# The two top weight blocks of each group of products in one transfer of 1 MB instead of two of 512 KB

## The reference

```python
proj = _rms(x, norm_mix) @ w_in          # 2048 x 4096: u | B | C | v
u, bg, cg, v = split(proj)
ya = pool_mixer(u)                       # trailing means over windows 2, 4, 8, 16, minus the token, times w_pool
yb = bg * conv3_causal(cg * v)
x = x + concat([ya, yb]) @ w_out
x = x + cross_attention(_rms(x, norm_attn), memory)
x = x + square(relu(_rms(x, norm_mlp) @ w_up)) @ w_down      # w_up 2048 x 8192, w_down 8192 x 2048
```

## Time and profile before

| | us |
|---|---|
| median of 3 runs | 2612.54 (2611.84 to 2614.34) |
| the profiled execution's own time | 2611.28 |
| its span, first to last instruction | 2609.6 |
| PE busy | 2569.2 (98%) |
| DVE busy | 1914.0 (73%) |
| ACT busy | 1107.6 (42%) |
| granted TensorE clock | 0.998 of full |

### The profile page before, as it was taken

The page is one execution under the profiler, slowest core; times in us unless marked ns, Lnnn a source line. Parts: engine busy times, 40 slices in busy tenths (PEclk is TensorE's granted clock), DMA queues, the critical chain, the costliest instruction groups (busy, mean ns, idle before and its releaser), DMA issues.

```text
span 2609.6 us, 47588 instructions
## 1 busy us (share of the span) xinstructions
PE 2569.2 (98%) x20056; PEld 2514.8 (96%) x20056; DVE 1914.0 (73%) x2342; ACT 1107.6 (42%) x1520; POOL 159.9 (6%) x253
## 2 busy tenths in 40 slices
PE   8999999999999999999999999999999999999997
PEld 8989999999999989989999999999999999999997
DVE  6789887763542243368888888888878888888888
ACT  6444444441321122234656555555533333333344
POOL 1000000010000010000011111000010000000000
PEclk9999999999999999999999999999999999999999
DMA  8673333362233455532566666565587555556542
GB/s 282 210 216 121 106 102 110 109 220 86 88 121 116 152 194 195 217 98 100 170 221 221 221 221 209 192 226 195 187 304 275 183 200 191 194 192 211 192 137 101
DMA packets 131856, 462.51 MB, mean 177 GB/s; under 512 B 11952, under 2 KB 18224, under 8 KB 120400
## 3 DMA queue, kind: packets, MB, share of 16 engines
q1 hardware_dynamic: 92448, 260.05, 30.8%
q0 software_dynamic: 39216, 199.71, 20.7%
HBM read 376.62 MB, written 83.09 MB: 176 GB/s over the span
## 4 chain that ended last, share of the span: by engine, by line
PE 92%; DVE 4%; issue 1%; DMA 1%; ACT 1%; SPq 0%; DVEq 0%; ACTq 0%
PE psum_main L2577 27%; PE psum_main L2187 25%; PE psum_side L2577 20%; PE psum_main L2322 7%; PE psum_side L2322 5%; PE psum_main L2298 3%; PE psum_main L2431 1%; DMA unit_raw<-weights 1%; PE psum_main L2503 1%; DVE unit_low L1865 1%; PE psum_side L2472 1%; PE psum_side L2396 1%; ACT unit_high L1161 1%; DMA mem_raw<-mem_t 0%; DVE residual L1998 0%
## 5 line engine op out<-in xcount | busy, mean ns | idle before, releaser
L1161 ACT ACTIVATE unit_high<-unit_raw 128x1024 fp32r<-128x1024 f32 x384 | 400.7, 1055 | 531.9 <-PE psum_main L2577 158.4
L1865 DVE TENSOR_TENSOR unit_low<-unit_raw,unit_high 128x1024 fp32r<-128x1024 f32 x384 | 468.0, 1222 | 108.2 <-ACT unit_high L1161 107.9
L2577 PE MATMUL psum_main<-tokens,unit_high 128*128 128x272 f32 x2048 | 388.5, 288 | 4.8 <-DVE hidden L1968 3.7
L2577 PE MATMUL psum_main<-hidden,unit_high 128*128 128x272 f32 x1984 | 377.0, 288 | 3.7 <-DVE residual L1998 2.7
L791 ACT ACTIVATE unit_high<-unit_raw 128x1024 fp32r<-128x1024 f32 x162 | 171.0, 1058 | 438.6 <-PE psum_main L2187 398.5
L2187 PE MATMUL psum_main<-inner_a,unit_high 128*128 128x272 f32 x2080 | 348.1, 289 | 2.8 <-issue 2.8
L2577 PEld LDWEIGHTS psum_main<-tokens,unit_high 128*128 128x128 f32 x2048 | 321.8, 189 | 5.6 <-DVE hidden L1968 4.4
L2577 PEld LDWEIGHTS psum_main<-hidden,unit_high 128*128 128x128 f32 x1984 | 312.1, 189 | 4.8 <-DVE residual L1998 3.7
L2187 PEld LDWEIGHTS psum_main<-inner_a,unit_high 128*128 128x128 f32 x2080 | 294.3, 188 | 6.1 <-issue 5.9
L2577 PE MATMUL psum_main<-tokens,unit_low 128*128 128x272 f32 x1024 | 295.1, 288 | 0.0
L2577 PE MATMUL psum_side<-tokens,unit_high 128*128 128x272 f32 x1536 | 293.1, 288 | 1.4 <-issue 0.8
(11 more groups left out here) (285 smaller groups left out, 4694.8 us busy)
## 6 DMA issues: line engine op xcount, KB each, us to landing
unit_raw<-weights SPq DMA_DIRECT2D x442, 512.0 KB, 4.3
hidden<-hidden_kept POOLq DMA_DIRECT2D x56, 1088.0 KB, 6.8
hidden_kept<-hidden_staged POOLq DMA_DIRECT2D x31, 1904.0 KB, 7.4
unit_sum<-weights SPq DMA_DIRECT2D x40, 512.0 KB, 3.6
residual<-x_t POOLq DMA_DIRECT2D x16, 544.0 KB, 5.9
residual_kept<-residual POOLq DMA_DIRECT2D x32, 272.0 KB, 5.0
cache_ring_t<-cache_k POOLq DMA_DIRECT2D x8, 1024.0 KB, 7.9
cache_low_a<-cache_v POOLq DMA_DIRECT2D x8, 1024.0 KB, 10.5
```

The source lines that it names most:

```text
L1161: act.activation(WHI[:, slot, :], raw, ACT.Copy).then_inc(mlp_high, 1)
L1865: dve.tensor_tensor(WLO[:, slot, :], raw, WHI[:, slot, :].bitcast(F32), ALU.subtract) \
L2577: ins = pe.matmul(bank, w[:, slot, col:col + P], moving[:, k, part, :], start=start and k == 0 and n == 0, stop=k == kk - 1 and n == 2, sk ...
```

## The change

In groups 1 to 15 of the projection and groups 1 to 31 of the MLP's up half, w11 and w12, which lie one behind the other in DRAM and go to neighbouring places of `RAW`, are fetched by one transfer of 1 MB. It is issued when both places are free, that is after the wait that w12 had. Only `block_raw[0]` counts it, so the ACT's conversion of w12 waits for that counter, and the numbers for `block_raw[1]` are adapted. Group 0 of each stage and the down half keep their separate transfers.

```diff
@@ input projection, SP
                     sp.wait_ge(in_sum, 4 * q)
-                    sp.dma_start(RAW[:, 0, :], w11).then_inc(block_raw[0], 16)
                     sp.wait_ge(in_ready, PRODUCTS * (q - 1) + 6)
-                    sp.dma_start(RAW[:, 1, :], w12).then_inc(block_raw[1], 16)
+                    sp.dma_start(RAW[:, 0:2, :], weights[u:u + 2].rearrange("u p n -> p u n")) \
+                        .then_inc(block_raw[0], 16)
@@ MLP, SP
                     sp.wait_ge(mlp_sum, 4 * q)
-                    sp.dma_start(into(q, RAW[:, 0, :]), w11).then_inc(block_raw[0], 16)
-                    sp.wait_ge(mlp_ready, PRODUCTS * (q - 1) + 6)
-                    sp.dma_start(into(q, RAW[:, 1, :]), w12).then_inc(block_raw[1], 16)
+                    if q < QUADS:
+                        u = MLP + q // HK * 4 * CH + 2 * (q % HK)
+                        sp.wait_ge(mlp_ready, PRODUCTS * (q - 1) + 6)
+                        sp.dma_start(RAW[:, 0:2, :], weights[u:u + 2].rearrange("u p n -> p u n")) \
+                            .then_inc(block_raw[0], 16)
+                    else:
+                        sp.dma_start(into(q, RAW[:, 0, :]), w11).then_inc(block_raw[0], 16)
+                        sp.wait_ge(mlp_ready, PRODUCTS * (q - 1) + 6)
+                        sp.dma_start(into(q, RAW[:, 1, :]), w12).then_inc(block_raw[1], 16)
@@ projection, ACT, high_in
+                elif source == 1 and q:
+                    act.wait_ge(block_raw[0], 16 * (q + 1))
@@ MLP, ACT, high
+                elif source == 1 and 0 < q < QUADS:
+                    act.wait_ge(block_raw[0], 16 * (IN_QUADS + q + 1))
+                elif source == 1:
+                    act.wait_ge(block_raw[1], 16 * (2 if q == 0 else q - QUADS + 3))
```

## The result

| | before | after |
|---|---|---|
| median, us | 2612.19 (4 runs) | 2642.34 (4 runs, 2639.9 to 2645.48) |
| profiled execution: own time, span | 2611.28, 2609.6 | 2645.48, 2643.8 |
| granted TensorE clock | 0.998 | 0.994 |

The changed kernel is slower by 1.16% (ratio 1.0116, 95% interval 1.0105 to 1.0128), 30 us. The forecast was 2636, 24 us. The profiled execution is the slowest of its four, and its span is 34.2 us above that of before.

What follows compares the result with a forecast made beforehand. Matmuls on the PE bound both stages, with little DVE reserve per group. Projection turns and first loss 21.4 us, projection end 1.4, MLP start 1.0 and up half nothing sum to 23.8: 2636 us median, range 2622 to 2658.

Steps and rivals of the forecast that it cites:

- closes a loop: Both stages: transfer, conversion, subtraction and the DVE's group feed the next issue; a turn over 21.05 us delays the PE.
- T + 1.11 + D: One turn: 1 MB issue to landing (T, 5.1 us), conversion and handover (1.11), DVE's share (D, 14.67 to 17.39).
- The up half stays inside: MLP's up half: 31 turns at -0.12 us against the PE's 21.05, so no loss.
- nothing else moves: Rest of the kernel: SP's queue, POOL's stores of hidden rows, the last product and the down half were to stay unaffected.
- t0: Moment when the low part of product 5 of the group before is made, when w12 was issued before the change.
- groups with a window of 2: Projection groups 13 and 14: turn excess of -0.17 us, so no loss.
- the first loss: Projection group 2: the low part of product 0 ready at 243.65, wanted by the PE at 242.5; 1.15 us.
- the end: End of the projection: DVE behind the PE and setting the pace, so about 1.4 us paid.
- the MLP's start: Where the MLP begins (1242 to 1262 us): w11 goes out later there too, 1.0 us allowed.
- Late landing: Rival, 0.17: T is 5.7; projection loses more and up-half turns exceed by 0.48 us; 45.9 us lost, 2658.
- Early landing: Rival, 0.14: an undisturbed 1 MB from the SP lands in 4.5 us, so the kernel takes 2627.
- No change: Rival, 0.07: the second half megabyte rides almost free, T 3.5; about 2.6 us lost, 2615, within 0.2%.

Runs made afterwards that it cites:

- the first experiment: Merged w11 and w12 transfer kept in the input projection only, MLP as in the kernel before; 2640.47 us, ratio 1.0118 to the kernel before.

## Why the prediction was right, and by how much it was off

The sign, the place and the mechanism were right.

*A wait put into the DVE's order closes a loop.* Shown: turns within 0.5 us of T + 1.11 + D with the measured T, and the loss down to 1.1 us when the mixers' work is moved out of the loop.

*The up half stays inside.* Shown twice: groups 21.05 us apart in the changed kernel's trace, and 0.13% for the up half alone. My -0.12 us of excess was -0.32 with T = 4.9.

*The term that was mis-sized is T in the projection.* I took 5.1 us for every group. The 13 transfers from group 1 to group 13 have a sum of 73.7 us, 7.4 above 13 x 5.1, and the turns from 236.27 to 537.57 are 27.6 us longer than 13 x 21.05; my turns gave 20.3. The two differences, 7.4 and 7.3, are nearly the same. Undisturbed the 1 MB is faster than I took it, 4.9, but I had looked for company only in the up half ("nothing else moves") and not in the projection, where POOL's store of the differences is issued about 1 us ahead of the t0 of content and value groups. The two groups with a window of 2, which I had at no loss, so lose 1.4 and 1.9 us.

*The ends.* From group 1's t0 to the mark behind the projection the loss is 30.1 us. The turns take 27.6 of it and leave 2.5, where I had 1.15 for the first loss and 1.4 for the end; the two can't be told apart here. For the MLP's start I had 1.0, and 1.2 were measured up to the end of the up half. The 1.3 us ahead of the MLP and the 2.6 behind it weren't in the forecast; a part of them is the PE's clock, which I had taken as full throughout.

*The rivals.* Late landing was right about T of 5.7 us or more in six of 15 groups of the projection, but with 4.9 in the up half its second part fell away, and with it the 46 us. Early landing is out (4.8 is the shortest of 46 and more). No change is out. The batching rule that I weighed (the Trainium skill, DMA: Bandwidth & Descriptors, section Measured) doesn't carry this case: two of 512 KB issued together and one of 1 MB are complete at the same 5.0 us. By the fit of the same page of the Trainium skill (section Anatomy of one DMA, measured on GpSimd's path) T would be 4.4 us, an estimate; the measured 4.9, from the SP's queue, is 0.5 above it.

## What to carry to other kernels

When two transfers become one, ask first who uses the first half: it now waits for the later of two free places and for the other half's bytes, and both delays enter the order of an engine that has only a few microseconds to spare per group. Add up one full turn from the transfer's issue through its consumers back to the issue; under the bounding engine's time the wait is free, above it every turn pays. And look at what the other queues issue at the same moment: here POOL's store and the one or two small transfers behind it, beside the 1 MB, were worth some 8 us.

## What the runs showed of the hardware that I had not expected

After some 2 us of idle time the PE's next product can be slow. Windows of 4 us of the kernel after, columns as in the earlier trace rows, behind content groups 5 and, for comparison, value group 2:

```profile
336.00:340.00 4.00, 1.67 (x14) 1.48 (x13) 2.51 (x3) 2.29 (x3) 0.00 (x0) 1.00 0.00 0
340.00:344.00 4.00, 4.00 (x22) 4.00 (x22) 2.87 (x4) 1.49 (x3) 0.00 (x0) 0.57 0.00 0
```
```profile
268.00:272.00 4.00, 2.68 (x21) 2.71 (x22) 4.00 (x6) 1.46 (x4) 0.00 (x0) 1.00 0.00 0
272.00:276.00 4.00, 4.00 (x33) 3.90 (x32) 2.87 (x3) 2.29 (x3) 0.00 (x0) 1.00 0.01 4
```

Where the PE had been idle 2.3 us, the granted clock of the next 4 us is 0.57, that is, 1.2 in place of 2.4 GHz for most of it, and they hold 22 matmuls instead of 34; behind value group 2, idle for 1.5 us (1.3 of it in the window shown), it is 1.00. This happens four times in the projection (at 244, 340, 432 and 500 us, each behind a landing of 6.2 us or more); in the one that the chain above shows, the product takes 4.7 us, 1.7 more.

The length of the idle time doesn't decide it alone. At 432 us the PE had been idle only 1.8 us. In the first experiment, with the merged transfer in the projection alone, it is idle 2.5 us behind content group 1 and keeps the full clock:

```profile
240.00:244.00 4.00, 1.51 (x12) 1.31 (x11) 1.54 (x3) 2.29 (x3) 0.00 (x0) 1.00 0.03 12
244.00:248.00 4.00, 4.00 (x33) 4.00 (x33) 3.43 (x4) 0.53 (x1) 0.00 (x0) 1.00 0.02 4
```

And the 2.8 us of idle time behind the projection were followed by the full clock in the kernel before and by half of it in the experiment with w11 alone behind low 5 (the windows shown there). What else decides it, no run here shows.

Most of the slow product isn't added to the total, since the DVE sets the pace there. Content group 1 gives a price: the turn behind it is 24.55 us in the first experiment, 0.25 below the loop's sum with its T of 6.3, and 25.17 in the changed kernel, 0.27 above the sum with 6.4. The turns of groups 1, 5, 9 and 12, the four with a slow product, are 0.3 to 0.5 us above the sum, all others 0.1 to 0.2 below. So a slow product costs its turn some 0.4 to 0.7 us, and the four some 2 to 3 of the 30 (an estimate from these turns). With POOL held the granted clock is 1.00 from 220 to 540 us, with no slow product, so a part of the 8 us won there is this.
